# First weights and columns in smaller pieces; head 0's row maxima between the last cache transposes

## The reference, cut to what matters

```
z = x @ w_in                                  # 520 tokens, 1024 -> 384 + 256 + 32 + 512 + 512
q_lat, kv_lat, k_pe, rec_x, rec_gate = split(z)
q = rmsnorm(q_lat) @ w_uq ; c_kv = rmsnorm(kv_lat) ; rotary on q_pe, k_pe
# prompt: causal attention over the prompt, 8 heads, blocks of 128 queries
s = (qn . kn + qp . kp) * SM ; p = softmax(causal(s)) ; o = p @ v
# decode: attention over the paged latent cache plus the new token, absorbed form
s_past = q_lat . c_past + q_pe . kpe_past ; s_new = the same with the new row
o_lat = softmax([s_past, s_new] * SM) @ [c_past, c_new] ; o = o_lat @ w_uv
# recurrent branch: causal conv of width 4, gates, h_t = a_t h_{t-1} + u_t, times gelu(rec_gate)
x1 = layernorm(ALPHA * x + [rmsnorm(att), rmsnorm(rec)] @ w_out)
y  = layernorm(ALPHA * x1 + moe(x1))          # 4 groups of 8 experts, top 1 group, top 2 experts
```

## Time and profile before

| | |
|---|---|
| three runs, median | 601.82 us (601.57 to 604.54) |
| profiled execution | 602.56 us, span 600.9 us |
| TensorE busy | 518.8 us, 86% of the span |
| VectorE, ScalarE, GpSimd busy | 373.2, 191.4, 134.0 us |
| read from memory, written | 160.12 MB, 21.23 MB |
| chain that ended last, by engine | PE 56%, DMA 26%, DVE 8%, ACT 7% |

### The profile page before, as it was taken

How to read it: one execution, slowest core, us unless ns; L and a number is a source line. 1 busy time by engine, 2 the same in 40 slices (tenths; PEclk the granted TensorE clock), 3 DMA queues, 4 the chain that set the end, 5 groups by cost and what they waited for, 6 DMA issues and landing times.

```text
span 600.9 us, 8960 instructions
## 1 busy us (share of the span) xinstructions
PE 518.8 (86%) x3296; PEld 281.0 (47%) x3296; DVE 373.2 (62%) x722; ACT 191.4 (32%) x356; POOL 134.0 (22%) x156
## 2 busy tenths in 40 slices
PE   5999999999979879899999898888887777767761
PEld 4887788874355443445556743333332222222220
DVE  1642059898933576652258666677886477666686
ACT  0100374214243644121142122444444244432340
POOL 1001054500025760000000201233323222221231
PEclk9999999999979999999999899999999899999997
DMA  9940008570606932001978599999999999999951
GB/s 302 405 155 6 1 1 331 213 269 1 279 5 230 395 116 87 2 1 59 417 290 342 180 420 406 409 396 419 415 415 411 419 418 419 415 415 418 401 193 43
DMA packets 34010, 157.95 MB, mean 263 GB/s; under 512 B 12680, under 2 KB 12680, under 8 KB 20016
## 3 DMA queue, kind: packets, MB, share of 16 engines
q1 hardware_dynamic: 20592, 127.46, 52.9%
q0 software_dynamic: 10752, 29.59, 13.0%
q10 hardware_dynamic: 2624, 0.34, 0.4%
HBM read 160.12 MB, written 21.23 MB: 302 GB/s over the span
## 4 chain that ended last, share of the span: by engine, by line
PE 56%; DMA 26%; DVE 8%; ACT 7%; issue 3%; SPq 0%; POOL 0%; DVEq 0%; POOLq 0%; ACTq 0%
DMA arena_o<-in_w_gu 19%; PE ps L489 17%; PE ps L748 8%; PE ps L962 8%; PE ps L985 4%; PE ps L651 3%; PE ps L589 2%; PE ps L635 2%; DVE arena_s L1477 2%; PE ps L672 2%; DMA first_rows<-arena_s,known 1%; DMA x_rows<-arena_s 1%; PE ps L555 1%; DMA known<-slot_table 1%; DMA slot_table<-arena_s 1%
## 5 line engine op out<-in xcount | busy, mean ns | idle before, releaser
L962 PE MATMUL ps<-arena_w,arena_s 128*64 128x512 f32 x368 | 109.2, 605 | 24.1 <-DMA arena_w<-in_w_gu 12.3
L489 PE MATMUL ps<-arena_w 128*128 128x260 f32 x416 | 94.5, 388 | 6.7 <-DMA arena_w<-in_w_in 6.2
L489 PEld LDWEIGHTS ps<-arena_w 128*128 128x128 f32 x416 | 79.7, 193 | 21.0 <-DMA arena_w<-in_w_in 6.2
L962 PEld LDWEIGHTS ps<-arena_w,arena_s 128*64 128x64 f32 x368 | 33.2, 139 | 96.9 <-issue 66.4
L985 PE MATMUL ps<-arena_w,cs 128*64 128x512 f32 x184 | 56.1, 615 | 20.8 <-ACT cs L1260 20.8
L748 PE MATMUL ps<-arena_o,arena_s 128*128 128x512 f32 x128 | 58.3, 601 | 1.6 <-DVE arena_s L1601 1.6
L962 PE MATMUL ps<-arena_o,arena_s 128*64 128x512 f32 x112 | 50.2, 595 | 0.0
L1477 DVE STREAM_TRANSPOSE arena_s<-arena_w 128x1024 f32<-128x1024 f32 x36 | 41.8, 1214 | 8.3 <-PE ps L589 8.2
L2150 POOL DMA_INDIRECT first_rows<-arena_s,known x15 | 18.0, 1202 | 113.9 <-ACT arena_s L1267 105.1
L1910 DVE TENSOR_TENSOR arena_s<-arena_s,ps 128x256 f32<-128x256 f32 x16 | 6.7, 421 | 56.5 <-ACT arena_s L1256 56.5
L985 PEld LDWEIGHTS ps<-arena_w,cs 128*64 128x64 f32 x184 | 16.0, 141 | 51.0 <-issue 30.3
(11 more groups left out here) (349 smaller groups left out, 897.3 us busy)
## 6 DMA issues: line engine op xcount, KB each, us to landing
arena_w<-in_w_gu SPq DMA_DIRECT2D x46, 1024.0 KB, 19.9
arena_w<-in_w_dn SPq DMA_DIRECT2D x23, 1024.0 KB, 19.9
arena_o<-in_w_gu SPq DMA_DIRECT2D x14, 1024.0 KB, 23.2
arena_o<-in_w_dn SPq DMA_DIRECT2D x7, 1024.0 KB, 23.8
arena_w<-in_w_in SPq DMA_DIRECT2D x13, 512.0 KB, 14.1
arena_o<-in_w_out SPq DMA_DIRECT2D x1, 4096.0 KB, 13.5
arena_s<-in_w_gu SPq DMA_DIRECT2D x4, 1024.0 KB, 8.1
arena_w<-in_xT SPq DMA_DIRECT2D x4, 520.0 KB, 6.7
```

Source lines behind the costliest of these rows:

```text
L489: last = mm(ps[rows, b + n, 0:HALF], lhs(k), rhs(k)[:, n * HALF:(n + 1) * HALF], start=(k == 0), stop=(k == ks - 1))
L962: last = mm(ps[64 * e:64 * e + 64, 2 + q, :], xgT[:, k, CAP * e:CAP * (e + 1)], gu_w[2 * slots + e][:, k, :], start=(k == 0), stop=(k == K ...
```

## The change

At the start SP sends the first half of chunk 0 (weight blocks 0 to 3) and single activation rows 0 and 1 ahead, then rows 2 and 3, then the other half of chunk 0, then the other rows. Unit 0 waits at k = 0, 1, 2, 4 and 6 for what it needs there. ScalarE's queue issues its first load as before and holds the other eight until activation row 1 has landed. In the middle VectorE takes head 0's first two row maxima behind the transposes of steps 6 and 7, its last two ahead of the cache's maximum, and head 1's first two ahead of `new_weights(0)`; ScalarE exponentiates head 0's blocks 1 and 0 ahead of the cache's scores; TensorE makes head 0's scores 1 and 0 ahead of the ninth cache product.

```diff
@@ -63,6 +63,7 @@
 CHUNK_OF = {**{U_RX + c: c for c in range(4)}, U_KV: 4, U_KV + 1: 5, **{U_Q[k]: 6 + k for k in range(3)},
             **{U_G[c]: 9 + c for c in range(4)}}
 N_CHUNKS = 13
+FIRST = (0, 1, 2, 4, 6)
 LAND_OF = [0, 1, 2, 3, 4, 5, 6, 6, 6, 7, 7, 7, 7]
 
 
@@ -361,10 +362,16 @@
 
             def chunk(c):
                 sp.dma_start(arena_w[:, c * D:(c + 1) * D], w_in[c]).then_inc(win_landed[LAND_OF[c]], 16)
-            sp.dma_start(xTv[:, 0:2, :], xT[:, 0:2, :]).then_inc(x_landed[0], 16)
-            chunk(0)
-            for n in range(1, 4):
-                sp.dma_start(xTv[:, 2 * n:2 * n + 2, :], xT[:, 2 * n:2 * n + 2, :]).then_inc(x_landed[n], 16)
+
+            def rows(a, b, done):
+                sp.dma_start(xTv[:, a:b, :], xT[:, a:b, :]).then_inc(done, 16)
+            sp.dma_start(arena_w[:, 0:D // 2], w_in[0][:, 0:D // 2]).then_inc(x_landed[0], 16)
+            rows(0, 1, x_landed[0])
+            rows(1, 2, x_landed[1])
+            rows(2, 4, win_landed[0])
+            sp.dma_start(arena_w[:, D // 2:D], w_in[0][:, D // 2:D]).then_inc(x_landed[2], 16)
+            rows(4, 6, x_landed[2])
+            rows(6, 8, x_landed[3])
             for c in range(1, 6):
                 chunk(c)
             sp.dma_start(arena_w[:, N_CHUNKS * D:W_X], w_kpe).then_inc(kpe_gates_landed, 16)
@@ -483,8 +490,8 @@
                     pe.wait_ge(evac[u % 4], u // 4)
                 b = 2 * (u % 4)
                 for k in range(ks):
-                    if u == 0 and k % 2 == 0:
-                        landed(pe, x_landed[k // 2])
+                    if u == 0 and k in FIRST:
+                        landed(pe, *((x_landed[0], 2), (x_landed[1], 1), (win_landed[0], 1), (x_landed[2], 2), (x_landed[3], 1))[FIRST.index(k)])
                     for n in range(2):
                         last = mm(ps[rows, b + n, 0:HALF], lhs(k), rhs(k)[:, n * HALF:(n + 1) * HALF],
                                   start=(k == 0), stop=(k == ks - 1))
@@ -492,7 +499,8 @@
 
             def project(u):
                 c = CHUNK_OF[u]
-                landed(pe, win_landed[LAND_OF[c]], LAND_OF.count(LAND_OF[c]))
+                if c > 0:
+                    landed(pe, win_landed[LAND_OF[c]], LAND_OF.count(LAND_OF[c]))
                 unit(u, lambda k: w_chunk[c][:, k, :], lambda k: xTv[:, k, :], KD)
 
             for u in range(U_RX, U_KPE):
@@ -701,9 +709,9 @@
             cache_scores(0, 6)
             new_scores()
             cache_scores(0, 7)
-            cache_scores(0, 8)
             scores(0, 1)
             scores(0, 0)
+            cache_scores(0, 8)
             pe.wait_ge(v_out, 4)
             pe.wait_ge(sn_out, 1)
             for s in range(NH):
@@ -1013,6 +1021,7 @@
             fn = nc.scalar.activation
 
             act.dma_start(vec[:, :], vecs).then_inc(params_landed, 16)
+            landed(act, x_landed[1])
             act.dma_start(cdec[:, :, 0:CONV - 1, :], conv_st).then_inc(params_landed, 16)
             act.dma_start(rst[:, :, :], rec_st).then_inc(params_landed, 16)
             act.dma_start(cs[64:128, :], cs_tab).then_inc(cs_landed, 16)
@@ -1146,9 +1155,9 @@
                 values_out(n)
             prob(0, 3)
             prob(0, 2)
-            cache_prob(0)
             prob(0, 1)
             prob(0, 0)
+            cache_prob(0)
             for s in range(NH):
                 more = s + 1 < NH
                 if more:
@@ -1549,27 +1558,31 @@
             last.then_inc(qs_done, 1)
             for c in range(2, NC):
                 transposed(0, c)
-            row_max(0, 3)
-            row_max(0, 2)
+                if c == 6:
+                    row_max(0, 3)
+                if c == 7:
+                    row_max(0, 2)
             dve.wait_ge(sn_ps, 1)
             step(V.tensor_copy(cn, ps[0:DEC, 7, P:P + KVL]))
             tt(snew[:, :, :], ps[:, 7, 0:NB * DEC].rearrange("p (b t) -> p b t", b=NB), smask[:, :, :], ALU.mult).then_inc(sn_out, 1)
             dve.wait_ge(sn_out, 1)
             step(V.tensor_reduce(nsn[:, :], snew[:, :, :], AX_X, ALU.add, negate=True))
             settle()
-            cache_max(0)
             inverse(0, 2)
             row_max(0, 1)
             row_max(0, 0)
+            cache_max(0)
+            inverse(0, 0)
+            row_max(1, 3)
+            row_max(1, 2)
             new_weights(0)
-            inverse(0, 0)
             for s in range(NH):
                 more = s + 1 < NH
-                if more:
+                if more and s > 0:
                     row_max(s + 1, 3)
                 if s == 1:
                     latent_out(0)
-                if more:
+                if more and s > 0:
                     row_max(s + 1, 2)
                 turned(dve, V.tensor_copy, s, 2)
                 if s == 0:
```

## The result

| | median of n runs, us | the kernel before beside it | ratio, 95% interval |
|---|---|---|---|
| first measurement | 599.63 (597.12 to 601.41, 16) | 602.83 (601.40 to 605.31, 16) | 0.9940, 0.9924 to 0.9956 |
| second | 598.32 (596.66 to 599.71, 6) | 602.22 (601.21 to 605.16, 23) | 0.9939, 0.9923 to 0.9954 |
| third | 599.36 (597.39 to 601.40, 6) | 604.28 (601.70 to 605.96, 17) | 0.9922, 0.9899 to 0.9944 |

What follows compares the result with a forecast made beforehand. One long chain of waits was taken to bound the kernel, with losses at the first transfer and around the cache's exponentials; 1.1 + 3.8 = 4.9 us off the 601.82 median gave 596.9, range 595.2 to 600.4.

Steps and rivals of the forecast that it cites:

- the line of 598.8: End to end: a time under 598.8 us would count as faster, given that a measurement tells about 3 us from no change.
- the forecast's own range: End to end: 595.8 to 598.2 us for the forecast case itself, which was given a chance of 0.58.
- rival 1: Middle: the clock falls in the new wait, so the gain is only 2.6 us, to 599.2; chance 0.15.
- The middle: Around the cache's exponentials: the reordering brings the cache values sooner by 3.8 us, bounds 1.5 to 4.1.
- the 0.3: Middle: 0.3 us left for copies of the turned exponentials closely following head 1's maxima and exponentials.
- The start: First transfers: TensorE starts 1.4 us sooner, at about 4.8, of which 1.1 is kept; bounds 0 and 1.4.
- rival 2: Start: the smaller transfer pieces land no sooner, so the gain is 3.8 us, to 598.0; chance 0.14.
- The held loads: Start, ScalarE's queue: the third small load lands near 16.6 us; the delay goes into idle times, cost 0.
- the gain is kept to the end if no later link hangs on a fixed time: After the middle: the whole 4.9 us reaches the end, the stream of expert weights starting as much sooner.
- own sign for being wrong: Later chain: wrong if the shift at the first expert product differs from that at the cache values by over 1.
- The new wait: TensorE ahead of the cache turns: a wait of 1.8 us, barely below the length expected to drop the clock.
- Rivals 3 and 4: Expert stage returns everything, 601.8, chance 0.08; or clock falls and cache value products stay at half speed, 606.2, chance 0.05.

Runs made afterwards that it cites:

- swap_alone: The kernel before with one exchange: on ScalarE head 0's exponentials of blocks 1 and 0 ahead of the cache's; 602.70 us, ratio 0.9976.
- maxima_back: The changed kernel with head 0's first two row maxima behind the last cache transpose again; 601.05 us, ratio 0.9954.
- start_alone: The kernel before with only the change's split first transfers and held small loads; 600.79 us, ratio 0.9989.
- changed_woven: The changed kernel with the router's thin products of the second and third tile woven between the output projection's dense products; 597.79 us, ratio 0.9930.
- head1_back: The changed kernel with head 1's first two row maxima behind the new token's weights again; 598.43 us, ratio 0.9918.
- middle_alone: The kernel before with only the reordering around the cache's exponentials, first transfers as before; 600.66 us, ratio 0.9962.
- changed_again: The changed kernel, unchanged, measured a second time; 598.32 us, ratio 0.9939.
- old_start_warm: The new middle with the old start, plus seven products of ones while TensorE waits for its first transfer; 599.86 us, ratio 0.9922.
- no_hold: The changed kernel with ScalarE's eight small loads issued at once again, not held for activation row 1; 600.66 us, ratio 0.9959.
- warm: The changed kernel with seven 128 x 128 products of ones ahead of unit 0; 598.19 us, ratio 0.9895.
- woven_warm: The changed kernel with seven products of ones ahead of unit 0 and the router's thin products woven into the output projection; 597.91 us, ratio 0.9903.
- changed_control: The changed kernel, unchanged, measured a third time; 599.36 us, ratio 0.9922.

## Why the prediction was right, and where not

**The time.** 599.63 lies inside the range 595.2 to 600.4, and "faster" came true by the ratio (0.9940, interval under 1), though not by the line of 598.8 that the prediction drew. The point 596.9 was 2.7 too low: 1.0 of it is the base, since the 601.82 of three runs became 602.83 over sixteen, and 1.7 is gain that did not come. Against the kernel before beside it the gain was 3.2 to 4.9 us, where 4.9 was forecast. That the range held is in part luck: 599.63 lies outside the forecast's own range, 595.8 to 598.2, and next to rival 1's 599.2, but not by rival 1's cause. In the first profile the clock stayed up in the middle and fell in the output projection, which the range had no term for.

**The middle: right, and a little more.** Every step can be read on the scale of before by adding the 1.07 that the k_pe unit came sooner: cache's maximum 163.95 (164.05 said), cache turns 168.58 (168.7), first cache value product (L636) 172.14 (172.4, and 172.7 with the 0.3). The stretch was 4.32 shorter in 7 of 7 profiles where the clock stayed up, 3.8 said. The turned copies cost none of the 0.3 left for them, and from the turns to the cache values' first product (L636) it took 3.56, not 3.7. What swap_alone and maxima_back add, in one profile each: the exchange on ScalarE needs VectorE's maxima ahead of it. With none of them moved TensorE waits 2.75 ahead of head 1's scores, with the first pair put back 2.65 ahead of the cache turns, and the clock fell behind both waits. TensorE's new order was not tried by itself.

**The start: mechanism right, the size not told apart from the forecast.** The sum took 1.1 between 0.7 and 1.3. With the new start the k_pe unit came on average at 49.66 (seven profiles: changed three times, start_alone, changed_woven, maxima_back, head1_back), with the old one at 50.59 (before, middle_alone, swap_alone): 0.93, but the two groups overlap (48.94 to 50.77 and 50.18 to 50.89). In runs, start_alone gave 0.7 (interval -0.1 to 1.4). Both take in the 1.1. What one number could not say is the spread: the level rose between 8.3 and 11.2 us in these ten profiles, whether TensorE had begun at 4.5 or at 6.6, and with the new start the k_pe unit followed it by about half:

```profile
L496 PE MATMUL ps<-arena_w x10: 383/638/803, 4.5 to 8.8; 128*128 128x260 f32 x10
```

is the changed kernel's first profile until 9 us (ns min/median/max, first and last start), and this is changed_again, same stretch:

```profile
L496 PE MATMUL ps<-arena_w x10: 641/641/802, 4.7 to 8.7; 128*128 128x260 f32 x10
```

One has reached 383 ns by then, the other not one record. That is what the Trainium skill, "TensorE: Matmul & The Clock Gate", Part 1, says of a watch that a kernel's start does not reset; the 500 ns either way that it gives are less than the spread here (8.3 to 11.2). The prediction had weighed it as both 0.7 and 1.3. The second limit, rows 2 and 3, was not in the sum: with the loads at once or the clock up early TensorE waited 0.90 to 1.59 for them. So rival 2 held for these rows, though not for the first piece: they were issued about 2.3 and landed 5.7 later, at 8.0, in the changed kernel's first profile, with 1296 KB queued up to their end (DMA issues from 2.2 to 2.75 us: what, queue, count, size, us to landing):

```profile
arena_w<-in_xT SPq DMA_DIRECT2D x1, 520.0 KB, 5.7
```

In the kernel before they took 5.8 from 1.84, to 7.6, with 1552 KB queued. Over all profiles they landed at 7.6 to 8.1 with the old start (four) and at 7.2 to 9.0 with the new one (ten): no sooner, with 256 KB less queued. (The 8.0 to 9.0 in the expectation of old_start_warm left out maxima_back, 7.2.)

**The held loads: right.** 18.4 instead of the 16.6 said for the landing, and no cost, as no_hold shows.

**The step that failed** is "the gain is kept to the end if no later link hangs on a fixed time". No link does, but the clock does not hang on a link either. Of 5.42 us at the second cache values, 3.73 were left behind the first fall in the output projection (288.5) and 2.04 behind the second (312.5). The prediction looked at the clock only at waits; these falls came behind thin products without a wait. They do not need the change: swap_alone, with VectorE's and TensorE's old order, had both (to experts: 71.99), and changed_again neither. But with the new middle they are not rare: the profiles with both falls, 599.66, 599.94 and 600.81, lie near the medians of their runs, 599.63, 599.36 and 600.66, and changed_again's 596.82 lies 1.5 below its own. The prediction's own sign for being wrong, a shift at the first expert product that differs by over 1, was met by this.

**Rival 1 is real.** The new wait measured 1.95, not 1.8, and so stood above the 1.80 that was to bound it. The clock fell behind it in 2 of 10 profiles that have it (warm, old_start_warm), at a price of 1.65 and not 2.4, because it was back by 172.4. It had a chance of 0.15. Rivals 3 and 4 did not happen: the clock was back before the eight-column products, which took 7.02 to 7.03 throughout.

**What stays open.** Several profiles with the new middle lost another 2.07 between the two cache values (100.9 instead of 98.85, clock at 0.50 for 6.8 us from about 220): 4 of 11, and 0 of 3 with the old middle. Three more (changed_again, changed_woven, woven_warm) fell there for 3.4 us, at a price of 0.22 at most. None of these seven fell in the output projection, and none of the four that fell there fell near 220; so a profile had at most one of the two, and why is not known. Whether the new middle makes such falls likelier can't be told from so few profiles, but the runs hint at it: without the 6.8 us at 0.50 near 167 the granted clock averaged over a span of 600.9 would rise by 0.0057, and beside the kernel before on the same chip it rose from 0.9795 (23 runs) to only 0.9823 (12 runs) in middle_alone and from 0.9811 (17) to 0.9815 (6) in changed_control. So part of the clock won there seems lost in other places. The average moves for other reasons too (start_alone, with the old middle, had 0.9812 over 12 runs beside the 0.9795), and how much time these falls cost no run shows.

## What to carry to other kernels

Take a long wait off TensorE and it gains twice: the wait, and the half-speed work behind it; here a wait cut only to 2.75 from 4.49 gained 0.75 of 4.32 us. Then look at where the clock falls next. Behind a transfer-bound start, look at the clock and at the next transfers before making the first ones smaller: an idle TensorE that multiplied ones brought the k_pe unit as early as the pieces did, in one profile. And compare several profiles stretch by stretch, and with the median of the runs: the first one showed half the gain lost in a stage that the change does not touch, the second did not, and only the medians say which of them is usual.

## What the runs showed of the hardware

- The granted clock fell to 0.50 with no idle time in TensorE's records ahead of it, behind 48 products of 8 and 36 columns, in 4 of 12 profiles, and not in the other 8 with the same instructions there.
- A wait of 1.95 us was followed by a fall in 2 of 10 profiles; the longer ones there (2.65, 2.75, 4.49) came with one in each of the four profiles that have them.
- Seven products of ones (3.35 us) brought records of 382 ns at 5.2 to 6.9 us in three profiles, instead of 7.8 to 11.2 in eleven.
- Activation row 1, one piece of 260 KB issued at 1.8 us, landed at 6.7 us in one profile of the changed kernel, and 0.8 later in changed_woven, whose start is the same, where TensorE waited 0.89 for it.
